# RWKV layers of a five-mixer transformer stack: paired low-rank factors, spread modulation sums, output products split in two

## The chip, the core and the metric

The kernel runs on one NeuronCore of a Trainium2 chip. The metric is the device time of one execution in microseconds (us). TensorE (PE in the profile) multiplies matrices into PSUM, eight banks of 128 partitions by 512 fp32. VectorE (DVE) and ScalarE (ACT) work on tiles of 128 partitions, and both read PSUM. GpSimd (POOL) and SyncE (SP) only issue DMAs here. Each engine works through its own list in order, and semaphores join the lists.

## What is computed

256 tokens of width 1024 go through four layers of feed-forward, mixer, feed-forward, and then through a second block. The mixers are RWKV-7 (layer 0), Mamba-2, windowed attention, and RWKV-7 again (layer 3; called RWKV layer 1 below, `j = 1`). Each of the 12 sublayers is modulated: shift, scale and gate come from `silu(c) @ ada_w`, a product of one row with a 1024 x 3072 matrix per sublayer. The change touches the two RWKV layers:

```python
dx = token_shift(h) - h
xr, xw, xk, xv, xa, xg = [h + dx * mu[j] for j in range(6)]
r = xr @ w_rkv[0];  k = xk @ w_rkv[1];  v = xv @ w_rkv[2]
w = -softplus(-(w0 + tanh(xw @ w1) @ w2)) - 0.5        # w1: 1024x64, w2: 64x1024
decay = exp(-exp(w))
a = sigmoid(a0 + (xa @ a1) @ a2)                       # a1, a2: rank 64
v = v + (v_first - v) * sigmoid(v0 + (xv @ v1) @ v2)   # rank 32, only j = 1
g = sigmoid(xg @ g1) @ g2                              # rank 160
kk = heads(k * k_k);  kk = kk / max(norm(kk), 1e-12)   # 16 heads of 64
k = k * (1 + (a - 1) * k_a)
# per token: state = state*decay + (state @ -kk)(kk*a)^T + v k^T;  y = state @ r
out = ((groupnorm(y) + sum(r*k*r_k) * v) * g) @ w_o
```

## The kernel before, in words

All activations lie transposed, as 8 tiles of 128 channels by 256 tokens. Weights come as 128x128 fp32 blocks, 24 blocks (1.5 MB) to a slot, in the order in which PE uses them, through a ring of three slots that SP fills (`stream_weights`, L397). Modulation weights come on POOL's queue (`ada_stream`, L410): a sublayer takes 16 chunks of 768 KB, there are two buffers, and a chunk is asked for when DVE has summed the one two places before it (`ada_sum`, L421: one 128x1536 multiply-add). RWKV layer 0 has two sublayers' chunks to sum, 32 of them; RWKV layer 1 has none left.

The **product phase** is written by hand on each engine (`rw_products` L931, `rw_act` L1184, `rw_vector` L1317). DVE forms six mixes of `h` and `dx`, 8 tiles each (`mix`, L1332), into two buffers, so mix `i` waits until the products of mix `i-2` are done. PE projects each mix (`project`, L751): 8 products of 128x256 to one output tile, in turn into three PSUM banks, which ACT empties. The order before is k, w1, the sums of squares of the key heads (`key_sums`), a1, the expansions w2 and a2 (`expand`), the spreading of the inverse norms (`spread_norms`), r, v, (v1), g1, (v2), g2. An expansion tile before is one product with 64 rows.

Within r, v and g2 PE also does the first step of a triangular inverse for four units (two chunks of 128 tokens by two halves of the heads): `open_near(u)` makes 128x128 products of the keys, DVE masks and sums them in two rounds (L1380 to L1386), PE replicates each round over the partitions (`spread_near(u, i)`, two 128x512 products), and then DVE runs 15 dependent pairs of small instructions (L1396, L1397). DVE's part is `base(u)`; it ends with the copy at L1398. The phase ends when PE transposes `v` and starts the bonus sums (128x256 products with `head_ones`).

The **chunk phase** goes over b = 0, 1 (chunks of 128 tokens) and hf = 0, 1 (halves of the heads). PE doubles the inverse to 32 and 64 with products of 128x128 (`wk_lx`, `wk_x32`, `wk_y32`, `wk_y64`), and makes the decayed products of r with a (`wk_ra`) and of k with r and kk (`wk_rk`), which DVE masks (L1517, L1520, L1530). Then a chain hands over six times: `wk_res` (PE) to ACT, `wk_sa`, ACT, `wk_across`, DVE (L1541), `wk_sa` again, ACT, and last the output `wk_out`, which for each half of the heads is 8 products k-part times v, 8 products rb times sa, and for b = 1 also 8 of r times state. DVE's L1468 is the first to read the output. `beside(n)` in `rw_vector` places modulation chunks in DVE's list.

Of the kernel before, what the change touches and what calls it, by code (L numbers as in the profile page):

```python
# [21 lines left out]
P = 128  # L22
# [16 lines left out]
RW_SLOTS, MB_SLOTS, SW_SLOTS, B2_SLOTS = 14, 22, 7, 30  # L39
# [39 lines left out]
def weight_slots(v):  # L79
    out = [slots_of([blocks_of(v["ada_w"][0][:, :ADA_COLS])])]  # L80
    for i in range(DEPTH):
        kind, j = i % 3, i // 3
        for s in range(2):
            if s == 1:
                if kind == 0:
                    w_r, w_k, w_v = v["rw_w_rkv"][j]
                    parts = [blocks_of(w_k)]
                    parts += [blocks_of(v[n][j]) for n in ("rw_w1", "rw_a1", "rw_w2", "rw_a2")]
                    parts += [blocks_of(w_r), blocks_of(w_v)]
# [26 lines left out]
    out.append(np.zeros_like(out[0][:-sum(len(o) for o in out) % RING]))  # L116
# [634 lines left out]
def project(k, pe, pr, x, kt, m=P, rows=P, before=None):  # L751

    bank = pr.q % RING
    if pr.q >= RING:
        pe.wait_ge(k.sem["evacuated"], pr.q - RING + 1)
    for t in range(kt):
        if before is not None:
            before(t)
        w = pr.take()
        pr.mm(k.psum[0:m, bank, 0:T], w[0:rows, 0:m], x(t), t == 0, t == kt - 1,  # L760
              k.sem["projected"] if t == kt - 1 else None)
    pr.q += 1

# [88 lines left out]
RW_MIXES = (2, 1, 4, 0, 3, 5)  # L852
# [15 lines left out]
class RwTiles:  # L868


    def __init__(self, k):
# [17 lines left out]
        self.norm = k.rms[0:16, :]  # L889
        self.one_less_ka = k.small[:, 0:8]  # L890
# [40 lines left out]
def rw_products(k, pe, pr, j, n):  # L931
    s, z, tiles = k.sem, RwTiles(k), rw_tiles(j)
    mm, q0 = pr.mm, pr.q
    mixes = iter(range(6))
# [10 lines left out]
    def full(beside=lambda m: None):  # L945
        kw, before = mixed()
        for m in range(KT):
            project(k, pe, pr, before=before if m == 0 else None, **kw)
            beside(m)
        return kw  # L950

    def expand(src, at, rows):
        evacuated(src)
        for m in range(KT):
            project(k, pe, pr, x=lambda t: z.lora[0:rows, at], kt=1, rows=rows)
# [1495 lines left out]
```

## Time and profile before

| | us |
|---|---|
| median of 3 runs | 3614.06 |
| the 3 runs | 3612.92 to 3615.4 |
| the profiled execution | 3613.66 |
| its span, first to last instruction | 3612.0 |
| mean granted TensorE clock, share of full | 0.923 |
| RWKV layer 0, first product of a mix to first product of w_o | 279.29 to 644.89 |
| RWKV layer 1, the same | 2443.84 to 2769.07 |

All times in rows are from the start of the span. The timeline view merges runs of equal instructions: start, duration of the run, engine, line of the kernel, operation, tile written <- tiles read, shapes (rows*columns of the weights, then the moving tile for PE), xcount, and in brackets how long the engine sat idle before and who released it. An fp32 product shows as two MATMUL records, so x16 is eight products.

### The profile page before, as it was taken

How to read it: one execution, taken by the hardware profiler on the slowest of the kernel's cores; microseconds unless marked ns; L12 is line 12 of the kernel's file. 1: busy time of each engine (PE TensorE's matmuls, PEld its weight loads, DVE VectorE, ACT ScalarE, POOL GpSimd, SP SyncE). 2: the span in 40 equal slices, each digit the busy share in tenths (PEclk: the TensorE clock that was granted, in tenths of full speed). 3: DMA queues.
4: the chain of work that ended last, by engine and by line, in shares of the span. 5: the costliest groups of instructions: out<-in, count | busy, mean ns of one | idle time of the engine just before them, and what ended most of it. 6: DMA issues, size and time to landing. Idle time of an engine off the chain costs nothing.

```text
span 3612.0 us, 57308 instructions
## 1 busy us (share of the span) xinstructions
PE 3322.7 (92%) x23680; PEld 3057.3 (85%) x23680; DVE 2050.8 (57%) x2856; ACT 1265.2 (35%) x1895; POOL 93.3 (3%) x180
## 2 busy tenths in 40 slices
PE   7995989999999799999995999999989999997898
PEld 7994768899999777999983899997678998856798
DVE  2656665566656963657655566655752545362444
ACT  2432111334435422435333344344121434331333
POOL 0000000000000000000000000000000000000000
PEclk9997997899999959999995999998897999988999
DMA  7755312465754603766642565752300443421343
GB/s 298 273 200 192 117 69 89 183 240 199 278 218 173 247 1 115 281 233 227 246 164 79 196 240 201 272 191 88 117 1 35 175 179 138 173 110 65 140 179 129
DMA packets 68758, 609.83 MB, mean 169 GB/s; under 512 B 7633, under 2 KB 7665, under 8 KB 30321
## 3 DMA queue, kind: packets, MB, share of 16 engines
q1 hardware_dynamic: 42912, 466.90, 34.5%
q0 software_dynamic: 25344, 138.42, 10.7%
q8 instruction: 126, 2.06, 0.2%
q10 hardware_dynamic: 336, 2.13, 0.1%
q14 instruction: 40, 0.32, 0.0%
HBM read 605.32 MB, written 2.10 MB: 168 GB/s over the span
## 4 chain that ended last, share of the span: by engine, by line
PE 53%; DVE 7%; ACT 2%; issue 1%; DMA 0%; DVEq 0%; ACTq 0%; POOLq 0%
PE psum L272 22%; PE psum L645 21%; PE psum L654 10%; DVE arena L574 1%; DVE rstd L572 1%; ACT arena L516 0%; DVE small L1948 0%; DVE arena L1940 0%; DVE wkv_base L1397 0%; DVE small L1396 0%; ACT up_part L618 0%; DVE arena L1961 0%; DVE h_part L582 0%; DMA ada_in<-in_ada_w 0%; DVE up_part L627 0%
## 5 line engine op out<-in xcount | busy, mean ns | idle before, releaser
L645 PE MATMUL psum<-h_part,up_part 128*128 128x256 f32 x9504 | 1183.0, 285 | 21.2 <-DVE h_part L582 20.4
L645 PEld LDWEIGHTS psum<-h_part,up_part 128*128 128x128 f32 x9504 | 1164.4, 193 | 23.3 <-issue 22.3
L654 PE MATMUL psum<-hidden_part,down_part 128*128 128x256 f32 x4752 | 601.3, 283 | 0.0
L272 PE MATMUL psum<-arena,weights 128*128 128x256 f32 (+3 forms) x2320 | 544.3, 396 | 46.2 <-issue 31.5
L654 PEld LDWEIGHTS psum<-hidden_part,down_part 128*128 128x128 f32 x4752 | 583.9, 192 | 0.0
L272 PEld LDWEIGHTS psum<-arena,weights 128*128 128x128 f32 (+3 forms) x2320 | 443.9, 194 | 149.1 <-issue 58.0
L627 DVE TENSOR_TENSOR up_part<-weights,up_part 128x2048 fp32r<-128x2048 f32 x198 | 453.0, 2288 | 135.4 <-ACT up_part L618 135.4
L618 ACT ACTIVATE up_part<-weights 128x2048 fp32r<-128x2048 f32 x198 | 376.3, 1900 | 42.8 <-DMA weights<-in_weights 41.8
L272 PE MATMUL psum<-arena 128*128 128x128 f32 (+8 forms) x2696 | 361.4, 334 | 27.5 <-DVE arena L1541 7.4
L698 ACT ACTIVATE arena<-psum 128x256 f32<-128x256 f32 x198 | 75.9, 383 | 859.3 <-PE psum L645 859.3
L272 PEld LDWEIGHTS psum<-arena 128*128 128x128 f32 (+3 forms) x2696 | 316.0, 217 | 66.7 <-issue 25.4
L729 DVE TENSOR_TENSOR arena<-arena,psum 128x256 f32<-128x256 f32 x198 | 83.2, 420 | 417.0 <-ACT arena L698 417.0
L272 PE MATMUL psum<-in_part,w_part 128*128 128x256 f32 x2352 | 292.6, 287 | 22.2 <-DVE w_part L793 9.7
L434 DVE SCALAR_TENSOR_TENSOR ada_sum<-ada_in,c_act,ada_sum 128x1536 f32<-128x1536 f32 x154 | 278.5, 1813 | 60.5 <-DMA ada_in<-in_ada_w 56.5
L272 PEld LDWEIGHTS psum<-in_part,w_part 128*128 128x128 f32 x2352 | 289.7, 196 | 25.1 <-issue 23.6
L724 DVE TENSOR_TENSOR down_part<-weights,down_part 128x1024 fp32r<-128x1024 f32 x198 | 241.2, 1218 | 20.6 <-ACT down_part L693 20.6
L272 PE MATMUL psum<-arena,consts 128*128 128x256 f32 (+6 forms) x636 | 195.5, 471 | 38.9 <-DVE small L1398 12.3
L693 ACT ACTIVATE down_part<-weights 128x1024 fp32r<-128x1024 f32 x198 | 206.5, 1043 | 15.1 <-PE psum L654 14.9
L272 PEld LDWEIGHTS psum<-arena,consts 128*128 128x128 f32 (+5 forms) x636 | 119.7, 218 | 96.8 <-issue 23.7
L824 ACT ACTIVATE arena<-psum 128x256 f32<-128x256 f32 (+2 forms) x139 | 54.0, 392 | 351.2 <-PE psum L272 351.2
L793 DVE TENSOR_TENSOR w_part<-weights,w_part 128x1024 fp32r<-128x1024 f32 x98 | 119.1, 1221 | 83.9 <-ACT w_part L787 83.9
L418 POOL DMA_DIRECT2D ada_in<-in_ada_w x174 | 91.9, 528 | 2273.9 <-DVE ada_sum L434 1273.8
(233 smaller groups left out, 1937.0 us busy)
## 6 DMA issues: line engine op xcount, KB each, us to landing
weights<-in_weights SPq DMA_DIRECT2D x294, 1536.0 KB, 6.2
ada_in<-in_ada_w POOLq DMA_DIRECT2D x176, 768.0 KB, 4.7
consts<-in_consts SPq DMA_DIRECT2D x1, 1844.0 KB, 9.3
x<-in_x SPq DMA_DIRECT2D x1, 1024.0 KB, 5.3
v_first<-arena ACTq DMA_DIRECT2D x1, 1024.0 KB, 3.9
arena<-v_first ACTq DMA_DIRECT2D x1, 1024.0 KB, 7.1
out<-x SPq DMA_DIRECT2D x1, 1024.0 KB, 3.9
params<-in_params SPq DMA_DIRECT2D x1, 458.0 KB, 3.3
```

Source lines behind the costliest of these rows:

```text
L272: ins = self.k.nc.tensor.matmul(out, lhsT=w, rhs=x, start=start, stop=stop, is_transpose=turn)
L418: pool.dma_start(k.ada_in[:, b], ada_w[g * 2 + b]).then_inc(k.ada_loaded[b], 16)
L434: ins = k.nc.vector.scalar_tensor_tensor(out, buf, c, out, ALU.mult, ALU.add)
L618: k.nc.scalar.activation(k.up_part[0][:, j % 2], k.weights[:, n % RING, 0:2 * KT * P], ACT.Copy)\
L627: k.nc.vector.tensor_tensor(k.up_part[1][:, j % 2], k.weights[:, n % RING, 0:2 * KT * P], k.up_part[0][:, j % 2].bitcast(FP32), ALU.subtra ...
L645: ins = mm(k.psum[:, j % RING, half * T:(half + 1) * T], lhsT=k.up_part[wp][:, j % 2, b:b + P], rhs=k.h_part[xp][:, t], start=t == 0 and n ...
L654: ins = mm(k.acc[:, d], lhsT=k.down_part[wp][:, j % 2, d * P:(d + 1) * P], rhs=k.hidden_part[xp][:, j % RING], start=start and d % 2 == 0 ...
L693: k.nc.scalar.activation(k.down_part[0][:, j % 2], k.weights[:, (n0 + j) % RING, 2 * KT * P:], copy)\
L698: k.nc.scalar.activation(k.silu[:, j % RING], k.psum[:, j % RING, 0:T], ACT.Silu)\
L724: v.tensor_tensor(k.down_part[1][:, j % 2], k.weights[:, (n0 + j) % RING, 2 * KT * P:], k.down_part[0][:, j % 2].bitcast(FP32), sub).then_ ...
L729: v.tensor_tensor(k.hidden[:, j % RING], k.silu[:, j % RING], k.psum[:, j % RING, T:2 * T], ALU.mult)\
L793: self.k.nc.vector.tensor_tensor(self.k.w_part[1][:, m % RING], self.weights(m)[1], self.k.w_part[0][:, m % RING].bitcast(FP32), ALU.subtr ...
```

## The change

1. `w1` and `a1` become the two column halves of the same 8 blocks, `w2` and `a2` the two row halves of 8 blocks, `v2` rows 32 to 63 of the second row block of `g2`. A RWKV layer takes 13 slots in place of 14. PE starts with `low_ranks` and `decays_and_rates`, which alternate between the halves; then come k, r, v. The two expansion products of an output tile go to two banks, taken as a pair.
2. `spread_norms` makes 8 products with 128 columns in place of 16 with 64, in r after tile 0.
3. The steps of the inverse move: `open_near` and `spread_near` stand at half tiles, unit 1 opens at the end of r, unit 2 in v, unit 3 after v.
4. DVE's modulation chunks of layer 0: before, 16 in one run after the second mix and 16 in the chunk phase. Now 7 between the tiles of k's scaling, 1 after the reciprocal, 3 after `base(0)`, 5 before `base(1)`, and 16 in the chunk phase at other places. In layer 1 `base(3)` goes ahead of the mixing of `v`.
5. Chunk phase: for b = 1 the bank pairs change roles; the k-part times v and the r times state products of the output go between `wk_sa` and `wk_across`, summed in PSUM ahead of rb times sa.

PE's list at the start of RWKV layer 0, before (`arena` holds the mixes, the low-rank results and the keys; `rw_mixed` counts DVE's mix tiles):

```order
L272 MATMUL psum<-arena,weights 128x256 [waits weights_loaded0,rw_mixed]
L272 MATMUL psum<-arena,weights 128x256 [waits rw_mixed] x7
L272 MATMUL psum<-arena,weights 128x256 x16
L272 MATMUL psum<-arena,weights 128x256 [waits weights_loaded1,evacuated]
L272 MATMUL psum<-arena,weights 128x256 x7
```

These are the products of k's first tiles. Now:

```order
L272 MATMUL psum<-arena,weights 64x256 [waits rw_mixed,weights_loaded0]
L272 MATMUL psum<-arena,weights 64x256 [waits rw_mixed] x15
L272 MATMUL psum<-arena,weights 128x256 [waits evacuated] x3
L272 MATMUL psum<-arena,weights 128x256
L272 MATMUL psum<-arena,weights 128x256 [waits evacuated]
L272 MATMUL psum<-arena,weights 128x256
```

The 64 products of k stood first and now stand behind 16 narrow ones and 16 expansions.

DVE's list of layer 0 between the end of `base(0)` (the COPY) and the first step of `base(1)` (the 128x512 TENSOR_TENSOR), before:

```order
L1398 COPY small<-consts 128x1 [waits dve_own]
L1332 SCALAR_TENSOR_TENSOR arena<-arena,params 128x256 [waits projected]
L1332 SCALAR_TENSOR_TENSOR arena<-arena,params 128x256 x7
L1404 SCALAR_TENSOR_TENSOR arena<-arena,params 128x256 [waits evacuated]
L1404 SCALAR_TENSOR_TENSOR arena<-arena,params 128x256 x7
L1407 TENSOR_TENSOR arena<-arena 128x2048 [waits rw_bonus_in]
L1408 TENSOR_TENSOR arena<-arena 128x2048
L1410 COPY small<-consts 128x1 [waits dve_own]
L1380 TENSOR_TENSOR arena<-psum,consts 128x512 [waits wk_near]
```

That is the last mix, the bonus products and two multiplications. Now:

```order
L434 SCALAR_TENSOR_TENSOR ada_sum<-ada_in,c_act,ada_sum 128x1536 [waits ada_summed,ada_loaded0]
L434 SCALAR_TENSOR_TENSOR ada_sum<-ada_in,c_act,ada_sum 128x1536 [waits ada_summed,ada_loaded1]
L434 SCALAR_TENSOR_TENSOR ada_sum<-ada_in,c_act,ada_sum 128x1536 [waits ada_summed,ada_loaded0]
L1378 SCALAR_TENSOR_TENSOR arena<-arena,params 128x256 [waits projected]
...
L1465 COPY small<-consts 128x1 [waits dve_own]
L434 SCALAR_TENSOR_TENSOR ada_sum<-ada_in,c_act,ada_sum 128x1536 [waits ada_summed,ada_loaded1]
L434 SCALAR_TENSOR_TENSOR ada_sum<-ada_in,c_act,ada_sum 128x1536 [waits ada_summed,ada_loaded0]
L434 SCALAR_TENSOR_TENSOR ada_sum<-ada_in,c_act,ada_sum 128x1536 [waits ada_summed,ada_loaded1]
L434 SCALAR_TENSOR_TENSOR ada_sum<-ada_in,c_act,ada_sum 128x1536 [waits ada_summed,ada_loaded0]
L434 SCALAR_TENSOR_TENSOR ada_sum<-ada_in,c_act,ada_sum 128x1536 [waits ada_summed,ada_loaded1]
L1434 TENSOR_TENSOR arena<-psum,consts 128x512 [waits wk_near]
```

Eight chunks now stand between the two. The third place is DVE's list in the chunk phase of layer 0, b = 0, from the mask of `wk_ra` to the read of `wk_across`, before:

```order
L1520 TENSOR_TENSOR arena<-psum,consts 128x1024 [waits wk_ra] x2
L1524 TENSOR_TENSOR arena<-arena,psum 128x1024 [waits wk_y,wk_y64] x2
L1530 TENSOR_TENSOR arena<-psum,consts 128x512 [waits wk_rk]
...
L434 SCALAR_TENSOR_TENSOR ada_sum<-ada_in,c_act,ada_sum 128x1536 [waits ada_summed,ada_loaded0]
L434 SCALAR_TENSOR_TENSOR ada_sum<-ada_in,c_act,ada_sum 128x1536 [waits ada_summed,ada_loaded1]
L1541 TENSOR_TENSOR arena<-arena,psum 64x8x64 [waits wk_res_read,wk_across]
```

Both chunks stand behind all masks. Now:

```order
L431 TENSOR_SCALAR ada_sum<-ada_in,c_act 128x1536 [waits ada_loaded1]
L1572 TENSOR_TENSOR arena<-psum,consts 128x1024 [waits wk_ra]
L434 SCALAR_TENSOR_TENSOR ada_sum<-ada_in,c_act,ada_sum 128x1536 [waits ada_summed,ada_loaded0]
L1572 TENSOR_TENSOR arena<-psum,consts 128x1024 [waits wk_ra]
L434 SCALAR_TENSOR_TENSOR ada_sum<-ada_in,c_act,ada_sum 128x1536 [waits ada_summed,ada_loaded1]
L1577 TENSOR_TENSOR arena<-arena,psum 128x1024 [waits wk_y,wk_y64] x2
...
L434 SCALAR_TENSOR_TENSOR ada_sum<-ada_in,c_act,ada_sum 128x1536 [waits ada_summed,ada_loaded0]
```

Chunks now stand ahead of and between the masks and adds; the last row shown is the one between the two rounds of `wk_rk`. The diff, cut to its core:

```diff
-RW_SLOTS, MB_SLOTS, SW_SLOTS, B2_SLOTS = 14, 22, 7, 30
+RW_SLOTS, MB_SLOTS, SW_SLOTS, B2_SLOTS = 13, 22, 7, 30
-RW_MIXES = (2, 1, 4, 0, 3, 5)
+RW_MIXES = (1, 4, 2, 0, 3, 5)
...
+    def pair():
+        if pr.q >= RING:
+            pe.wait_ge(s["evacuated"], pr.q - RING + 2)
+        banks = pr.q % RING, (pr.q + 1) % RING
+        pr.q += 2
+        return banks
+
+    def low_ranks():
+        banks, w = pair(), pr.take(KT)
+        for t in range(KT):
+            for i in range(2):
+                pe.wait_ge(s["rw_mixed"], 48 * j + KT * i + t + 1)
+                mm(k.psum[z.rows(i), banks[i], 0:T], w[:, t * P + 64 * i:t * P + 64 * i + 64], z.mix[i][:, t],
+                   t == 0, t == KT - 1, s["projected"] if t == KT - 1 else None)
+
+    def decays_and_rates():
         for m in range(KT):
-            project(k, pe, pr, x=lambda t: z.lora[0:rows, at], kt=1, rows=rows)
+            banks, w = pair(), pr.take()
+            for i in range(2):
+                if m == 0:
+                    evacuated(("w1", "a1")[i])
+                mm(k.psum[:, banks[i], 0:T], w[z.rows(i)], z.lora[z.rows(i), 1], True, True, s["projected"])
...
-    def beside_v(m):
-        if m == 2:
+        if (m, half) == (7, 1):
             open_near(1)
-        if m == 4:
+
+    def beside_v(m, half):
+        if (m, half) == (1, 1):
             spread_near(1, 0)
...
         for hf in range(2):
             at("wk_res_read", hf)
             for m in range(8):
-                mm(k.psum[0:64, 4 * hf + 2, m * 64:(m + 1) * 64], z.y[hf][0:64, m, 0:64], z.res[hf][0:64, m],
+                mm(k.psum[0:64, bank(hf, 2), m * 64:(m + 1) * 64], z.y[hf][0:64, m, 0:64], z.res[hf][0:64, m],
                    True, True, s["wk_sa"] if m == 7 else None)
+            for p in range(4):
+                for i in range(2):
+                    part(out(hf, i, p), lhsT=z.kl[hf][:, 4 * i + p, 0], rhs=z.vt[:, b, 4 * hf + p, z.rows(i)],
+                         start=p == 0 and (b == 1 or i == 0), stop=False, skip_group_check=True)
...
     mix(1)
-    if j == 0:
-        for i in range(ADA_STEPS):
-            ada_sum(k, dve, 2, i)
     mix(2)
...
+    for t in range(KT):
+        evacuated("k", t)
+        dve.wait_ge(s["rw_k_factor"], KT * j + t + 1)
+        ins = v.tensor_tensor(z.k[:, t], z.k[:, t], z.k_factor[:, t], mult)
+        if t < KT - 1:
+            beside()
+    ins.then_inc(s["rw_k_scaled"], 1)
+    dve.wait_ge(s["rw_key_sums"], j + 1)
+    v.tensor_scalar(z.norm, k.psum[0:16, 3, 0:T], 1e-24, None, ALU.max).then_inc(s["rw_norm"], 1)
+    mix(4)
+    dve.wait_ge(s["rw_norm_root"], j + 1)
+    v.reciprocal(z.norm, z.norm).then_inc(s["rw_norm"], 1)
+    beside()
```

## Rows read from the trace of the kernel before

**Rows 1.** The page's first line.
```profile
span 3612.0 us, 57308 instructions
```
**Rows 2.** Timeline of PE in the product phase of RWKV layer 0.
```profile
346.18 7.04 PE L272 MATMUL psum<-arena,weights 128*64 128x256 f32 x22 [28.94 <-issue]
...
379.28 1.16 PE L272 MATMUL psum<-arena 64*128 64x128 f32 x16
...
437.14 0.62 PE L272 MATMUL psum<-consts,mod_rows 24*128 24x24 f32 x2 [4.81 <-DVE mod_rows L483]
...
485.09 6.13 PE L272 MATMUL psum<-arena,consts 128*128 128x256 f32 x16 [6.33 <-DVE small L1398]
```
**Rows 3.** Timeline of DVE, modulation chunks of layer 0: first run, second run.
```profile
286.43 1.94 DVE L431 TENSOR_SCALAR ada_sum<-ada_in,c_act 128x1536 f32<-128x1536 f32 x2
...
525.72 3.53 DVE L434 SCALAR_TENSOR_TENSOR ada_sum<-ada_in,c_act,ada_sum 128x1536 f32<-128x1536 f32 x2
...
539.94 1.82 DVE L434 SCALAR_TENSOR_TENSOR ada_sum<-ada_in,c_act,ada_sum 128x1536 f32<-128x1536 f32 x1 [1.33 <-DMA ada_in<-in_ada_w]
```
**Rows 4.** Timelines of layer 0: two narrow PE groups, and ACT emptying expansions.
```profile
313.62 3.63 PE L272 MATMUL psum<-arena,consts 128*16 128x256 f32 x16
...
359.82 3.67 PE L272 MATMUL psum<-rms,consts 16*64 16x256 f32 x32
...
353.46 6.94 ACT L824 ACTIVATE arena<-psum,params 128x256 f32<-128x256 f32 x16
```
**Rows 5.** Stretches: us, busy by engine, then granted PE clock, DMA share, GB/s.
```profile
535.00:545.00 10.00, 6.34 (x60) 6.10 (x60) 6.48 (x7) 0.98 (x2) 1.58 (x3) 0.50 0.56 202
...
2490.00:2500.00 10.00, 10.00 (x34) 6.58 (x34) 7.57 (x12) 6.92 (x16) 0.00 (x0) 0.50 0.00 0
...
2730.00:2740.00 10.00, 10.00 (x98) 9.77 (x98) 1.38 (x2) 2.37 (x4) 0.00 (x0) 0.50 0.01 2
```
**Rows 6.** Timeline of DVE in and after base(0) of layer 0.
```profile
382.27 1.43 DVE L1386 TENSOR_TENSOR arena<-small,consts 128x256 f32<-128x256 f32 x4
...
394.54 0.28 DVE L1396 TENSOR_TENSOR small<-psum,wkv_base 128x120 f32<-128x120 f32 x1 [3.60 <-PE psum L272]
...
402.31 0.15 DVE L1398 COPY small<-consts 128x1 f32<-128x1 f32 x1
402.38 3.25 DVE L1332 SCALAR_TENSOR_TENSOR arena<-arena,params 128x256 f32<-128x256 f32 x8
...
408.83 2.29 DVE L1407 TENSOR_TENSOR arena<-arena 128x2048 f32<-128x2048 f32 x1
```
**Rows 7.** Timeline of PE, three tiles of g2 in layer 0.
```profile
460.90 3.83 PE L272 MATMUL psum<-arena,weights 128*128 128x256 f32 x12 [0.46 <-ACT arena L824]
```
**Rows 8.** Timeline of PE in the product phase of RWKV layer 1.
```profile
2519.34 1.16 PE L272 MATMUL psum<-arena 64*128 64x128 f32 x16
...
2623.97 6.77 PE L272 MATMUL psum<-arena,consts 128*128 128x256 f32 x16 [5.96 <-DVE small L1398]
```
**Rows 9.** Timelines of the chunk phase of layer 1, DVE and PE.
```profile
2660.44 4.86 DVE L1530 TENSOR_TENSOR arena<-psum,consts 128x512 f32<-128x512 f32 x8
...
2761.01 0.69 DVE L1468 TENSOR_REDUCE small<-psum 128x8 f32<-128x512 f32 x1 [8.46 <-PE psum L272]
...
2664.17 21.21 PE L272 MATMUL psum<-arena 128*128 128x64 f32 x288 [1.25 <-DVE arena L1530]
```
**Rows 10.** Timelines of the chunk phase of layer 0, DVE and PE.
```profile
514.04 1.22 DVE L1517 TENSOR_TENSOR arena<-psum,consts 128x1024 f32<-128x1024 f32 x1 [0.56 <-PE psum L272]
...
520.93 4.87 DVE L1530 TENSOR_TENSOR arena<-psum,consts 128x512 f32<-128x512 f32 x8
...
555.32 0.69 DVE L1468 TENSOR_REDUCE small<-psum 128x8 f32<-128x512 f32 x1 [4.05 <-PE psum L272]
...
636.84 0.69 DVE L1468 TENSOR_REDUCE small<-psum 128x8 f32<-128x512 f32 x1 [8.46 <-PE psum L272]
...
538.66 18.60 PE L272 MATMUL psum<-arena 64*64 64x64 f32 x176 [5.41 <-DVE arena L1541]
```

More of the change, by code:

```diff
@@ L745, in ffn_residual_wait, with project @@
     return done
-def project(k, pe, pr, x, kt, m=P, rows=P, before=None):
+def project(k, pe, pr, x, kt, m=P, rows=P, before=None, at=0, beside=lambda half: None):
     bank = pr.q % RING
@@ L966, in spread_norms @@
         for t in range(KT):
-            for i in range(2):
-                mm(k.acc[64 * i:64 * i + 64, t], k.const("ident", 16)[:, 2 * t + i:2 * t + i + 1].to_broadcast([16, 64]),
-                   z.norm, True, True, s["rw_norm_spread"] if t == KT - 1 and i else None)
+            mm(k.acc[:, t], z.norm_rows[:, t * P:(t + 1) * P], z.norm, True, True, s["rw_norm_spread"] if t == KT - 1 else None)
     def near_products(u, bank, signal):
@@ L1169, in rw_products @@
                 for i in range(2):
[L1170 to L1177 removed]
+                    ins = part(out(hf, i, p), lhsT=z.rb[hf][:, 4 * i + p], rhs=z.sa[hf][:, 4 * i + p], start=False,
+                               stop=True, skip_group_check=True)
+            ins.then_inc(s["wk_out"], 1)
     for hf in range(2):
@@ L1237, in rw_act @@
         ev.tile(z.g[:, m], f.Copy)
+        if j:
+            ev.tile(z.v_share[:, m], f.Sigmoid, bias=k.param("rw_v0", m))
     for i in range(4):
@@ L1341, in rw_vector, with beside @@
         mix(0, range(4 * half, 4 * half + 4))
+    units = [(u, i) for u in (2, 3) for i in range(ADA_STEPS)] if j == 0 else []
+    def beside(count=1):
+        for _ in range(count if units else 0):
+            u, i = units.pop(0)
+            ada_sum(k, dve, u, i)
     mix(1)
-    if j == 0:
-        for i in range(ADA_STEPS):
-            ada_sum(k, dve, 2, i)
     mix(2)
-    dve.wait_ge(s["rw_key_sums"], j + 1)
-    v.tensor_scalar(z.norm, k.psum[0:16, 3, 0:T], 1e-24, None, ALU.max).then_inc(s["rw_norm"], 1)
     mix(3)
-    dve.wait_ge(s["rw_norm_root"], j + 1)
-    v.reciprocal(z.norm, z.norm).then_inc(s["rw_norm"], 1)
-    mix(4)
-    evacuated("w2")
+    evacuated("wa2")
     for t in range(KT):
@@ L1400, in rw_vector @@
     base(0)
+    beside(3)
     mix(5)
@@ L1410, in rw_vector @@
     v.tensor_copy(k.small[:, 102:103], k.const("eps")).then_inc(s["rw_keys"], 1)
+    beside(5)
     base(1)
+    base(2)
     if j == 0:
         mod_rows(k, dve, 2)
-    base(2)
-    if j == 0:
-        mod_columns(k, dve, own, 2)
     projected("v1" if j else "v")
@@ L1426, in rw_vector @@
         v.tensor_tensor(z.v, z.v, z.v_first, add).then_inc(s["rw_v_mixed"], 1)
-    base(3)
+    if j == 0:
+        mod_columns(k, dve, own, 2)
     evacuated("v")
@@ L1435, in rw_vector @@
     projected("end")
-    def pair(hf, which):
-        return k.psum[:, 4 * hf + 2 * which:4 * hf + 2 * which + 2, :].rearrange("p i (n c) -> p (i n) c", n=4)
     def each(name, m=8):
         return k.const(name).unsqueeze(1).to_broadcast([P, m, P])
-    chunk = iter(range(ADA_STEPS if j == 0 else 0))
-    def beside(count=1):
-        for _ in range(count):
-            i = next(chunk, None)
-            if i is not None:
-                ada_sum(k, dve, 3, i)
     for b in range(2):
```

256 lines of the change are left out of this document (137 added, 119 removed).

## The prediction, made before the changed kernel ran

> **What bounds the kernel now.** I read the page's first line for the span [rows 1], then the timelines of the two RWKV layers, since everything else keeps its instructions. In a product phase PE sets the end except where it waits for DVE. In layer 0 four such waits matter: 28.94 us before a1's products, because 16 modulation chunks stand in DVE's list ahead of the mix that a1's turn depends on; 4.81 us for the modulation rows; some 3 us at a spread; 6.33 us for the end of `base(3)` [rows 2]. The chunks go at DMA pace: the run begins at 286.43 and takes 59 us for 16 sums of 1.82 us or less [rows 3]. In the chunk phases I compare layer 1, which has no chunks, with layer 0. From the bonus sums to the last `wk_out` layer 1 takes 2761.01 - 2623.97 = 137.0 us [rows 8, 9], layer 0 636.84 - 485.09 = 151.8 us [rows 2, 10]. So 32 chunks cost layer 0 about 29 us in one phase and 14.7 in the other. The question is what they cost at their new places.
>
> **Layer 0, front.** Before, the first near products run at 379.28 [rows 2]. Now: PE can begin `low_ranks` at 279.3, but its second product needs DVE's ninth mix tile, which I put at 283.7 (mix tiles take 3.25/8 = 0.41 us [rows 6]). The 16 products alternate between column halves. That halves run side by side is seen where 16 products into halves take 3.67 us and 8 whole ones 3.63 [rows 4]; bounds are 0.43 us a pair at the high clock and 0.86 at the low one. PE comes from waiting, so I take 0.86: done at 290.7. Tanh, copy and a table load add about 2.2. Then 8 pairs of expansions: ACT needs 6.94/16 = 0.43 us a tile [rows 4], and a pair waits until the tile before last is emptied, so a pair costs 0.43 + 0.05 + (0.43 or 0.86) + 0.1 = 1.0 to 1.44 us; at 1.44 the last is emptied at 304.4, and k's products start at 303.5. They take 27.6 us and 2.5 more for a cold start: 333.6; key sums 3.6.
>
> DVE meanwhile does the cumulative sums (about 10 us) and then the scaling with 7 chunks between. Chunks arrive about 5.3 us after the sum two places earlier, so the loop ends at DMA pace, at 337 to 341; I take 339. From there: 0.5 for the norm, 3.25 for mix 4 [rows 6], 1.73 reciprocal, 3.45 spreading, 24 products of r 10.35: near products at **358.5**, 20.8 us earlier.
>
> **Layer 0, middle.** `base(0)` now takes near 1.2 + first half 3.3 (to the end of the row at 382.27 less 380.4) or the 3.45 of r's tile 4, spread 1.7, half a tile 1.7, spread 1.7, then 7.9 from the first small step to the copy (394.54 to 402.46) [rows 6]: 17.8, so 376.3. Then 3 chunks. A burst with two chunks loaded goes as in the second run: from 525.72 the third sum ends 8.8 us later and the fifth at 541.76, 16.0 us later [rows 3]. So 8.8, then mix 5 3.25, the bonus products 3.25, two multiplications 2.3 each, 11.2 in all [rows 6], then 5 chunks 16.0: `base(1)` starts at 412.3 and its first half is ready at 415.5. PE has done near(1) and two tiles of v by 384.9 and waits for just that: **30.6 us idle**. The wait of 28.94 is not gone but stands at another place. This is the step that I trust most: each length has a row.
>
> From there (S = 415.5): spread, half tile, spread, 20 products, near(2): S + 13.8; `base(2)` ends S + 31.7; v with 24 modulation sums ends S + 34.1; DVE's `ended` and first half of `base(3)` S + 39.6; PE's g1 and transposes S + 43.4; two tiles of g2. A tile of g2 costs 3.83/3 = 1.28 us [rows 7], not 2 x 0.43. Spread(3,0), three tiles, spread(3,1), 8.1 of small steps, modulation columns, transposes: S + 63.9. After the long idle PE runs slow for a while; after a wait of 5.41 us the stretch read 0.50 [rows 5, 10], the lower of the clock's two levels, 1.2 GHz. I add 3. Bonus sums at 482.5, before 485.09 [rows 2]: **-2.6** (range -9 to +3).
>
> Of switching between whole tiles and 32-row halves the Trainium skill ("TensorEngine Tiling (Array Packing)", Key Properties) says that changing the mode drains TensorE. The 1.28 us of rows 7 agrees; without drains 5 tiles would cost 2 us less in each layer.
>
> **Layer 1, product phase.** No chunks. Low ranks bound by DVE's mixes, done at 2451.5; expansions 8.2 to 11.5 (before, with single 64-row products, PE fell to 0.50 in 2490 to 2500 [rows 5]); near products at 2512 to 2518, I take 2515.5, before 2519.34 [rows 8]. `base(0)` 17.8, then 11.2 and 3.3: first spread of unit 1 at 2547.8, while PE is there at 2542: a new wait of about 5.8 us, and 4 us of low clock behind it. Then as above without modulation sums but with v1 (3.6), and with tiles of g2 and v2 in pairs of banks at 1.7 us; `base(3)` ends about 61.2 + 4 later. Only then does DVE mix v, three 128x2048 operations of 2.29 [rows 6], and PE's transposes wait for it. Bonus sums at 2622 to 2626, before 2623.97 [rows 8]: **0** (range -6 to +5). What the shared blocks save (16 expansions to 8 places, 8 products of v2 beside g2's) is lost to the pair rule, the new wait and the later v.
>
> The skill's same page ("PSUM Bottleneck") says that tiling speeds TensorE but not the emptying of PSUM. Rows 4 agree for the expansions: by products alone 8 pairs would be 3.4 us.
>
> **Layer 1, chunk phase.** Does taking a third to two thirds of the output products ahead help? Only if PE waits there. For b = 0 PE's merged row has 288 records in 21.21 us with no idle [rows 9]. By single handovers I find the same: from sa on, ACT and DVE are each done while PE works on the other half of the heads. For b = 1 it is busy 10.00 of 10 at the low clock [rows 5]. The same products in another order end at the same time: **0** (-3 to +1). The swapped banks cost nothing: near(2) no longer waits for the state, but PE is busy until then.
>
> **Layer 0, chunk phase.** Now DVE has one chunk after lx1, two at `wk_ra`, and one between the rounds of `wk_rk`. Before, masks end at 515.26 (lx1) and 525.8 (rk) [rows 10]. Now: 1.0 us chunk, mask, 1.82 chunk, mask at 520.4, chunk 521.5 (its DMA) to 523.3, two adds to 525.7, four rk masks to 528.1, chunk to 529.9, four to 532.3: 6.5 us late. Behind it the chunks between the two across reads are one, not two: before, from the rk masks to the last output 29.5 us (525.8 to 555.32), of which 10.7 are over layer 1's pattern of 18.1 and 0.7 in the start. After: 6.5 + 1 + about 7.5 of low clock, since PE is idle from 526.3 to 531.2 and the wait of 5.41 brought 0.50 before: 15.0, so +4.3 (bounds -3.2 warm, +9.8 all slow). For b = 1: chunks add 7.3 to the end of rk (594.3 to 601.6), and 1.8 of the old delay between the across reads goes: +5.5. Sum **+9.8**.
>
> **Other parts.** Two weight slots fewer: PE waits for no weights in these phases, so 0. Key order, `spread_norms` with 8 products: in the front. The feed-forward layers are unchanged.
>
> **Sum.** -2.6 + 0 + 0 + 9.8 = +7.2 on the profiled 3613.66 (0.4 below the median) gives 3620.9; on the median 3614.06, **3621**.
>
> **Rivals.** *A, the clock holds and DMAs are prompt* (faster): low ranks and expansions at the high clock bring layer 0 -8 and layer 1 -6, the chunk phase 6.5 + 1 - 10.7 + 5.5 = +2.3: 3602. For it: layer 1's b = 0 ran 288 records in 21.21 us, 0.15 us a product, so such products alone do not bring the clock down [rows 9]; against: [rows 5]. *B, the forecast*, with its own range 3612 to 3631. *C, the low clock through* (the other way, slower): from the point at which PE's waits pass about 5 us it stays at 1.2 GHz for the whole handover chain and in g2: layer 0 +2, layer 1 +5, chunk phase +9.8 + 6.5: 3637. *D, the halves do not run side by side* when weights are 128 rows deep: low ranks +6.9 and +3.4, expansions +3.4 to +6.9 in all: 3637 and up; rows 4 speak against it. I make no rival of chunks that are fetched ahead (the 16.0 would be 9.1): there are two buffers, and the third chunk needs a sum to free one.
>
> **How the numbers follow.** A measurement tells about 0.2% (7.2 us) from no change, so the borders are 3606.8 and 3621.3. A 0.20, all faster. B 0.57: 0.32 within, 0.25 slower, since its middle lies at the border. C 0.16 and D 0.07, slower. Together faster 0.20, same 0.32, slower 0.48. The range of 8 in 10 reaches just past the middles of A and C, 3600 to 3639; half of A and half of C and D lie outside.
>
> **What the profile after would show.** A PE wait near 385 to 415 of about 30 us, released by DVE's first step of `base(1)`, in place of the 28.94; in layer 1 the same of 6. Near products of layer 0 at 358. Rk masks of layer 0 ending 6 to 7 us later after `wk_lx`. PE without idle between sa and the output in layer 1, b = 0, and last `wk_out` 137 us after the bonus sums. If the middle wait is under 20 us, or the chunk phase of layer 1 is more than 3 us shorter, my working is wrong.

## The result, and the profile after

The changed kernel takes 3649.97 us (median of 4 runs, 3645.0 to 3653.32); the kernel before took 3613.49 (4 runs, 3611.95 to 3615.4). The ratio is 1.010, 95% interval 1.0082 to 1.0117: slower by some 36 us, where the forecast was 3621 and its range ended at 3639. The profiled execution, the fastest of the four, took 3645.0 us with a span of 3643.3, which is 31.3 over the span of before [rows 1]. By stretch, each from PE's first product of the one step to that of the next:

| stretch | before | after | difference | forecast |
|---|---|---|---|---|
| start to the first mix product of layer 0 | 279.3 | 279.8 | +0.5 | 0 |
| layer 0, to the bonus sums | 205.8 | 216.2 | +10.4 | -2.6 |
| layer 0, bonus sums to `w_o` | 159.8 | 178.7 | +18.9 | +9.8 |
| to the first mix product of layer 1 | 1799.0 | 1794.9 | -4.0 | 0 |
| layer 1, to the bonus sums | 180.1 | 188.0 | +7.9 | 0 |
| layer 1, bonus sums to `w_o` | 145.1 | 143.7 | -1.4 | 0 |
| `w_o` of layer 1 to the end | 842.9 | 841.9 | -1.0 | 0 |

The page of after begins:

```profile
span 3643.3 us, 57258 instructions
```

The timeline of PE in the product phase of layer 0 (columns as ahead of the prediction), which answers to [rows 2]:

```profile
346.48 7.19 PE L272 MATMUL psum<-rms,arena 16*128 16x256 f32 x16 [7.60 <-DVE rms L1421]
353.60 12.54 PE L272 MATMUL psum<-arena,weights 128*128 128x256 f32 x48
366.07 1.16 PE L272 MATMUL psum<-arena 64*128 64x128 f32 x16
384.74 1.16 PE L272 MATMUL psum<-arena 64*128 64x128 f32 x16
...
427.54 3.78 PE L272 MATMUL psum<-arena,consts 128*128 128x512 f32 x4 [34.53 <-DVE arena L1440]
...
496.03 4.33 PE L272 MATMUL psum<-arena,consts 128*128 128x256 f32 x16
```

The 28.94 us wait of before is gone, and one of 34.53 stands behind v's second tile, released by DVE's first step of `base(1)`. What DVE does in that time is in its timeline:

```profile
384.14 3.55 DVE L434 SCALAR_TENSOR_TENSOR ada_sum<-ada_in,c_act,ada_sum 128x1536 f32<-128x1536 f32 x2
396.09 1.82 DVE L434 SCALAR_TENSOR_TENSOR ada_sum<-ada_in,c_act,ada_sum 128x1536 f32<-128x1536 f32 x1 [8.40 <-DMA ada_in<-in_ada_w]
397.83 3.25 DVE L1378 SCALAR_TENSOR_TENSOR arena<-arena,params 128x256 f32<-128x256 f32 x8
...
408.88 3.55 DVE L434 SCALAR_TENSOR_TENSOR ada_sum<-ada_in,c_act,ada_sum 128x1536 f32<-128x1536 f32 x2
415.79 1.82 DVE L434 SCALAR_TENSOR_TENSOR ada_sum<-ada_in,c_act,ada_sum 128x1536 f32<-128x1536 f32 x1 [3.36 <-DMA ada_in<-in_ada_w]
```

These are eight chunks on a path on which PE waits: 13.7 us for three of them and 15.4 for five.

In the chunk phase of layer 0, b = 0, the timelines of DVE and PE around the masks of `wk_rk`, to be held against [rows 10]:

```profile
530.48 1.82 DVE L434 SCALAR_TENSOR_TENSOR ada_sum<-ada_in,c_act,ada_sum 128x1536 f32<-128x1536 f32 x1 [1.16 <-DMA ada_in<-in_ada_w]
532.21 2.35 DVE L1577 TENSOR_TENSOR arena<-arena,psum 128x1024 f32<-128x1024 f32 x2
534.47 2.48 DVE L1583 TENSOR_TENSOR arena<-psum,consts 128x512 f32<-128x512 f32 x4
536.87 1.81 DVE L434 SCALAR_TENSOR_TENSOR ada_sum<-ada_in,c_act,ada_sum 128x1536 f32<-128x1536 f32 x1
538.59 2.48 DVE L1583 TENSOR_TENSOR arena<-psum,consts 128x512 f32<-128x512 f32 x4
```

```profile
533.48 2.87 PE L272 MATMUL psum<-arena 64*128 64x256 f32 x16 [2.66 <-DVE arena L1577]
539.93 8.99 PE L272 MATMUL psum<-arena 128*128 128x64 f32 x48 [3.58 <-DVE arena L1583]
548.85 3.67 PE L1187 MATMUL psum<-arena 128*128 128x64 f32 x16
```

The last line is the value part, now ahead of `wk_across`. The stretches give the granted clock (columns as in [rows 5]):

```profile
534.00:541.00 7.00, 3.42 (x19) 2.19 (x16) 7.00 (x11) 0.00 (x0) 0.53 (x1) 0.57 0.41 130
541.00:577.00 36.00, 35.69 (x259) 34.32 (x260) 12.20 (x26) 4.84 (x9) 1.58 (x3) 0.50 0.25 85
```

PE is busy 35.69 of 36.00 us at 0.50 of full clock. In layer 1, b = 0, where no chunk stands, products of the same kinds run at 1.00:

```profile
2694.94:2716.00 21.06, 21.06 (x278) 20.38 (x280) 8.53 (x26) 5.04 (x10) 0.00 (x0) 1.00 0.01 2
```

### The profile page after: what moved, and what is told of

The parts are those of the page before. It is cut to its first block, busy times and chain, and to the rows that moved or that the text cites. A ratio compares the mean times of both kernels' runs of the same rounds, so it can differ in the third digit from the quotient of the medians.

```text
span 3643.3 us, 57258 instructions
## 1 busy us (share of the span) xinstructions
PE 3323.1 (91%) x23648; PEld 3056.1 (84%) x23648; DVE 2053.4 (56%) x2870; ACT 1266.4 (35%) x1897; POOL 93.4 (3%) x180
## 4 chain that ended last, share of the span: by engine, by line
PE 53%; DVE 6%; ACT 2%; issue 1%; DMA 0%; DVEq 0%; ACTq 0%; POOLq 0%
PE psum L272 21%; PE psum L645 21%; PE psum L654 10%; DVE arena L574 1%; DVE rstd L572 1%; ACT arena L516 0%; DVE small L2001 0%; DVE arena L1993 0%; PE psum L1187 0%; PE psum L1214 0%; ACT up_part L618 0%; DVE arena L2014 0%; DVE h_part L582 0%; DVE arena L1378 0%; DMA ada_in<-in_ada_w 0%
## 5 line engine op out<-in xcount | busy, mean ns | idle before, releaser
L272 PE MATMUL psum<-arena,weights 128*128 128x256 f32 (+2 forms) x2320 | 530.4, 400 | 34.1 <-DVE arena L1378 17.2
L272 PEld LDWEIGHTS psum<-arena,weights 128*128 128x128 f32 (+2 forms) x2320 | 429.5, 195 | 138.6 <-issue 36.8
L272 PE MATMUL psum<-arena 128*128 128x128 f32 (+8 forms) x2376 | 315.4, 334 | 29.7 <-DVE arena L1583 9.6
L272 PEld LDWEIGHTS psum<-arena 128*128 128x128 f32 (+3 forms) x2376 | 270.3, 214 | 67.4 <-issue 23.4
L827 ACT ACTIVATE arena<-psum 128x256 f32<-128x256 f32 (+3 forms) x136 | 53.2, 393 | 424.3 <-PE psum L272 424.3
```

Source lines behind the costliest of these rows:

```text
L272: ins = self.k.nc.tensor.matmul(out, lhsT=w, rhs=x, start=start, stop=stop, is_transpose=turn)
```

## The experiments

There are two theories on the whole of the difference. **P**: the places of the 32 chunks in DVE's list cost most of it. **S** or **V**: the new structure does (halves and shared blocks, the later mixing of `v`; in the chunk phase the value part summed early and the swapped banks). Each kernel's marks come from PE's timeline of its profiled execution: "L0 near" and "L0 bonus" are the starts of layer 0's first near products and of its bonus sums in us from the start of the span, the next three columns are durations.

| kernel | span | L0 near | L0 bonus | L0 bonus to `w_o` | L1 first to bonus | L1 bonus to `w_o` | median (range) of its runs |
|---|---|---|---|---|---|---|---|
| before | 3612.0 | 379.3 | 485.1 | 159.8 | 180.1 | 145.1 | 3613.5 (3612.0 to 3615.4) |
| after | 3643.3 | 366.1 | 496.0 | 178.7 | 188.0 | 143.7 | 3650.0 (3645.0 to 3653.3) |
| n_before | 3560.6 | 348.2 | 454.1 | 145.0 | 177.9 | 145.0 | 3570.9 (3555.9 to 3584.5) |
| n_after | 3580.9 | 357.2 | 458.3 | 145.8 | 188.0 | 146.2 | 3579.6 (3577.8 to 3592.4) |
| place | 3626.1 | 365.5 | 496.0 | 159.2 | 188.0 | 143.7 | 3627.8 (3624.1 to 3631.5) |
| late | 3644.8 | 367.8 | 497.9 | 174.3 | 188.0 | 144.3 | 3643.3 (3640.4 to 3646.5) |
| late_place | 3629.9 | 366.6 | 496.7 | 161.8 | 188.0 | 144.3 | 3630.5 (3624.9 to 3633.1) |
| inbase | 3623.1 | 366.6 | 477.2 | 176.5 | 187.9 | 143.7 | 3628.8 (3624.8 to 3634.3) |
| mixpair | 3640.2 | 363.6 | 493.8 | 178.1 | 186.2 | 143.7 | 3645.0 (3641.9 to 3646.6) |
| b_place | 3641.2 | 381.2 | 487.0 | 173.7 | 179.9 | 159.3 | 3642.9 (3637.8 to 3652.2) |
| best1 | 3597.4 | 363.7 | 467.0 | 159.2 | 179.8 | 143.9 | 3592.5 (3588.6 to 3599.1) |
| b_best | 3599.8 | 356.1 | 459.0 | 164.8 | 174.5 | 159.1 | 3598.1 (3581.3 to 3601.4) |
| best2 | 3592.8 | 353.8 | 457.0 | 156.8 | 177.1 | 160.9 | 3594.5 (3581.2 to 3596.4) |
| before_2 | 3605.7 | 380.0 | 485.8 | 164.2 | 171.3 | 145.0 | (one run) 3607.4 |

The kernel before ran again beside each later group of kernels, with medians of 3618.2, 3614.3, 3625.3 and 3611.6 and single runs from 3604 to 3653. That spread is wider than what most single edits are worth, so the edits are judged by the marks, and the reason of the spread has a part of its own below. The marks scatter too: in two executions of the same kernel (`before`, `before_2`) layer 0's chunk phase differs by 4.4 us and layer 1's product phase by 8.8.

**The chunks taken out of both kernels.**

```diff
-    if unit >= NORMS:
+    if unit >= NORMS or unit in (2, 3):
         return
```

Units above 3 move down by two in the stream and in the waits. Both kernels leave out the modulation of two sublayers.

> The changed kernel with the 32 modulation chunks of RWKV layer 0 left out: neither fetched nor summed, so the modulation of two sublayers is wrong and the time is that of the rest. Theory P (the chunks' places are the main cause): layer 0 then looks like layer 1; the 34.53 us wait falls to about 6, the chunk phase from the bonus sums to the first product of w_o falls from 178.7 to about 144, and the front ends at ACT's and PE's pace; span about 3575. Rival S (the new structure is the cause: column halves, shared banks, the later mixing of v, the early value sums): the span stays 25 us or more above that of the same removal in the kernel before.

> The kernel before with the same 32 chunks left out (same part of the computation missing). Theory P: the 28.94 us wait goes and the chunk phase falls from 159.8 to about 145: span about 3568, so the two kernels without chunks differ by 5 to 13 us, which is what layer 1 shows (+6.5) once more or less. Rival S: they differ by 25 us or more.

From layer 0's first product to its `w_o` `n_before` and `n_after` take some 320 and 325 us, 5 apart; with chunks they are 29.3 apart (10.4 + 18.9). So the chunks' places cost some 24 of layer 0's 29, as P has it. The middle wait of PE in `n_after` is 6.14 us, as in layer 1 of after:

```profile
390.32 3.78 PE L272 MATMUL psum<-arena,consts 128*128 128x512 f32 x4 [6.14 <-DVE arena L1442]
```

S is not nothing, though. Layer 1 of `n_after` is 11.3 us longer than that of `n_before` (188.0 + 146.2 against 177.9 + 145.0), and the spans are 20.3 apart, more than the 5 to 13 expected, while the medians are 8.7 apart; two of the four runs of `n_before` (3579.5 and 3584.5) lie 17 us or more above the other two. The structure costs 5 in layer 0 and 6.5 to 11 in layer 1; of the rest of the 20.3, 4 lie outside the two layers, where no instruction differs.

**The chunk phase: places against early sums.** `place` puts the chunks back, `late` sums the value part at the end, `late_place` does both, and `b_place` gives the kernel before the new places alone.

```diff
-        beside()            # behind both first masks
+            beside()        # behind each
...
-            beside()        # behind each mask of wk_ra; one more behind the second wk_lx
...
-            beside()        # behind each round of wk_rk
+        beside(2)           # behind both rounds
...
-            beside()        # behind each across read
+            beside(2)
```

> The changed kernel with DVE's 16 chunks of the chunk phase put back where they stood before (one after each first mask, two behind all rk masks, two after each across read); the product phase and PE's order stay as changed. Theory P: from the bonus sums to the first product of w_o 178.7 falls to 160 to 163, the PE wait of 2.66 ahead of the last rk products is gone; span 3625 to 3628. Rival V (the value part summed early and the swapped banks are the cause in this phase, because PE stays at the lower clock): less than 4 us gained, 3640 to 3645.

> The changed kernel with the value part of the outputs (and r times state) summed at the end of the chain as before; the chunks stay at their new places. Theory P: within 3 us of the changed kernel (3640 to 3648), since PE has the same products and is busy or is waiting for masks that are late. Rival V: layer 0's phase falls by 9 or more, span 3635 or less.

> The kernel before with one part of the change alone: DVE's 16 chunks of the chunk phase at the places of the changed kernel. Theory P: from the bonus sums to the first product of w_o of layer 0 159.8 rises to 170 to 178, span 3622 to 3630. Rival V (these places cost only together with the value part summed early): less than 4 us.

> The changed kernel with both parts of its chunk phase undone: chunks at the old places and the value part of the outputs summed at the end of the chain. Against the run with the old places alone it shows what the early sums are worth where DVE's masks are on time. Theory E0 (PE is busy or slow there anyway, the order of the same products is worth nothing): bonus sums to first product of w_o 158 to 162 in place of 159.2. Rival E1 (the early sums fill the waits for the across reads, 3.16 and 2.04 us): 163 to 166, and layer 1 unchanged at 144.

The phase falls from 178.7 to 159.2 with the old places and rises from 159.8 to 173.7 when the kernel before gets the new ones: P, in both directions. The span of `b_place`, 3641.2, still missed the 3622 to 3630 expected, because layer 1's chunk phase took 159.3 us in it where it took 145.1 (below).

The worth of the early sums is less clear. `late` ends at 174.3, 4.4 us less than after; its span is 1.5 above that of after, its median 6.7 below. At the old places `late_place` takes 161.8 against 159.2, in the range of E0 (158 to 162) and not in that of E1. PE's timeline of `late_place` and then of `place` around the wait for the across reads shows the mechanism that E1 named:

```profile
548.55 23.64 PE L272 MATMUL psum<-arena 64*64 64x64 f32 x176 [5.75 <-DVE arena L1589]
```

```profile
543.38 3.07 PE L272 MATMUL psum<-arena 64*64 64x64 f32 x48
549.61 3.92 PE L272 MATMUL psum<-arena 64*64 64x64 f32 x48 [3.16 <-DVE arena L1592]
```

The sums fill 2.6 us of a wait of 5.75. That the net 2.6 is the same 2.6 is not shown. In b = 0, from the first product of `wk_rk` to the end of the output, `place` takes 32.4 us and `late_place` 38.0, but the two executions of the kernel before, which sum late, take 32.6 and 37.4, and in b = 1 `place` loses 2.8 us again. Over the whole phase the three executions with early sums at the old places (`place`, `best1`, `best2`) take 156.8 to 159.2 and the four with late sums (`before`, `before_2`, `late_place`, `b_best`) 159.8 to 164.8. So the early sums probably bring something where DVE's masks are on time; how much is open. In layer 1 the two kernels are 0.6 us apart.

**The middle of the product phase.** `inbase` puts the eight chunks where DVE waits inside `base`:

```diff
             if i:
+                beside((2, 2, 1, 0)[u])
                 dve.wait_ge(s["wk_spread"], 2 * UNITS * j + 2 * u + 1)
...
         own.of(v.tensor_copy(x, k.const("same_row").unsqueeze(1).to_broadcast([P, 8, 16])))
+        beside((1, 1, 1, 0)[u])
...
     base(0)
-    beside(3)
...
-    beside(5)
     base(1)
```

> The changed kernel with the eight chunks between base(0) and base(1) put inside base(0), base(1) and base(2), where DVE waits for PE to spread a round (three, three and two chunks); nothing else moved. Theory P: PE's wait ahead of the first spread of unit 1 falls from 34.53 us to 5 to 9, as in RWKV layer 1 (6.14), bonus sums of layer 0 at 466 to 472 in place of 496.03, span 3614 to 3620. Rival M (the chunks then wait for their DMA inside base and lengthen it by as much): bonus sums after 480, span 3627 or more.

PE's wait falls from 34.53 to 5.88, and the bonus sums come 18.9 us earlier, at 477.2, between the ranges of P (466 to 472) and M (after 480); the span, 3623.1, lies between theirs too. PE's timeline:

```profile
405.57 3.65 PE L272 MATMUL psum<-arena,consts 128*128 128x512 f32 x4 [5.88 <-DVE arena L1441]
```

The timeline of DVE shows the price:

```profile
372.65 3.55 DVE L434 SCALAR_TENSOR_TENSOR ada_sum<-ada_in,c_act,ada_sum 128x1536 f32<-128x1536 f32 x2
376.11 1.42 DVE L1441 TENSOR_TENSOR arena<-small,consts 128x256 f32<-128x256 f32 x4
381.72 1.82 DVE L434 SCALAR_TENSOR_TENSOR ada_sum<-ada_in,c_act,ada_sum 128x1536 f32<-128x1536 f32 x1 [4.05 <-issue]
```

With half tiles DVE waited only 0.58 and 2.01 us inside `base(0)` of the changed kernel, less than the 5.4 of three sums, and the third chunk, which POOL asked for at 375.12, comes 6.6 us later. `base(0)` takes 23.5 us in place of 16.9, `base(1)` 21.5 in place of 19.1, `base(2)` 18.0 in place of 16.8. M was half right: the chunks lengthen base, but by 10 us in all, where ahead of `base(1)` they took 29.

**The front.** `mixpair` makes the first two mixes in turn:

```diff
-        mix(0, range(4 * half, 4 * half + 4))
+        for t in range(4 * half, 4 * half + 4):
+            mix(0, (t,))
+            mix(1, (t,))
```

> The changed kernel with DVE making the first two mixes tile by tile in turn, so that PE's alternating low-rank products do not wait for the ninth of 16 mix tiles. Theory L (the late second product costs the front of both layers): low ranks of layer 1 done 3 to 4 us earlier and its bonus sums too; layer 0 gains 0 to 3, since its k loop ends at DMA pace; span 3636 to 3641. Rival C (the front is bound by the granted clock and by ACT): less than 1 us in either layer, span 3642 to 3645.

Counted from the layer's first product, the low ranks are done 2.7 us sooner in layer 0 and 1.8 in layer 1. The near products gain the same, 2.8 and 1.9, and so do layer 1's bonus sums, 1.9 (expected 3 to 4). So L is right in kind and too large: the late second product costs layer 1 some 2 us of its 7.9. The span is 3.1 shorter, the end of the expected range that lies nearest to no gain.

**Towards a faster kernel.** `best1` joins `place`, `inbase` and `mixpair`, lets `base(1)`, the last mix and `base(2)` follow `base(0)` directly, and spreads the norms a tile later. `best2` also moves the front chunks. `b_best` leaves the kernel before as it is but for the product-phase chunks (and `mod_sums`, which needs them):

```diff
-        for i in range(ADA_STEPS):
-            ada_sum(k, dve, 2, i)
+    early_sums(8)           # behind mix(1); 2 more behind mix(4), 3 in base(0), 3 in base(1)
```

> The changed kernel with what the runs so far point to: the chunk-phase chunks at the places of before, the eight middle ones inside base as in the run above, base(1) and base(2) directly behind base(0) with the last mix between, the first two mixes in turn, spread_norms one tile of r later. Theory P: bonus sums of layer 0 at 455 to 463, of layer 1 12 to 15 us earlier than in the changed kernel relative to its first product, chunk phase 159, span 3582 to 3595, faster than both kernels. Rival D (DVE becomes the bound, since bonus products and two multiplications now stand ahead of base(3)): bonus sums of layer 0 at 470 or later, span 3600 to 3612.

> The kernel before with nothing but its product-phase chunks moved in DVE's list: 8 behind the second mix in place of 16, 2 behind mix 4, 3 inside each of base(0) and base(1), where DVE waits for a spread; mod_sums and the turn of the modulation rows stand later in v. Theory P (where the chunks stand is worth more than all the rest of the change): the wait of 28.94 falls to 0 to 5, near products of layer 0 at 350 to 356, bonus sums at 458 to 466, span 3583 to 3593, level with the best version built on the changed kernel. Rival S (the shared blocks and the half-tile places bring something by themselves): 3600 or more.

> The best version so far with its front chunks moved: 3 behind the fourth mix, where DVE waited 8.5 us for ACT, 3 in the k loop in place of 7, 2 behind the reciprocal. Theory Q (the k loop ended at DMA pace, with waits of 4.1, 1.2, 4.9 and 4.6 us in it): the loop ends with the products of k, near products of layer 0 at 357 to 360 in place of 363.65, and the span falls by 3 to 6. Rival R (the two chunks behind the reciprocal take what the loop gives): within 2 us.

`best1` takes 3592.54 us, 0.992 of before (0.989 to 0.996): bonus sums of layer 0 at 467.0 (P had 455 to 463), layer 1's 8.2 us earlier (12 to 15 expected); the span, 3597.4, is 2 over the expected range. `best2` takes 3594.51 (0.991, 0.988 to 0.994) and `b_best` 3598.06 (0.992, 0.989 to 0.995). The lowest runs of the two are 3581.2 and 3581.3. The span of `b_best`, 3599.8, missed P's range (3583 to 3593) and is just under S's 3600, but 14 us of it are layer 1's chunk phase again (159.1 against 145.0), and its bonus sums at 459.0 are in P's range. So nothing here shows that the shared blocks, halves and early sums bring anything that the kernel before does not get from moving its chunks alone. In `best2` the k loop no longer holds PE: near products at 353.8 against 363.7, more than the 4 to 7 that Q had; the span falls by 4.6 only, because layer 1's chunk phase took 17.1 us more in this execution (below).

> The kernel before, unchanged, profiled once more, to see where its runs differ by up to 30 us. Theory K: one of the stretches of 128x64 and 64x64 products runs at the lower clock where it ran at the higher one in the first profile, with the same instructions and no wait more; each such stretch is worth 10 to 15 us. Rival: a longer wait for a DMA.

K is right on the mechanism: the waits of PE and DVE on DMAs are the same in kind, and 69.8 us in `before_2` against 71.5 in `before`. Its layer 1 reaches the bonus sums 8.8 us sooner, because products that ran at 0.50 now run near 1.00. The expansions of w2 and a2 in PE's timeline of `before` and then of `before_2`:

```profile
2485.89 10.60 PE L272 MATMUL psum<-arena,weights 64*128 64x256 f32 x26 [0.76 <-ACT arena L824]
```

```profile
2491.28 5.90 PE L272 MATMUL psum<-arena,weights 64*128 64x256 f32 x26 [0.77 <-ACT arena L824]
```

This is not a stretch of the kind that K named, and is worth 6.6 us up to the near products. One of that kind went the other way: the 176 records of 64x64 products that took 18.60 us in `before` [rows 10] take 23.40 in `before_2` (its timeline), and layer 0's chunk phase is 4.4 us longer (164.2 against 159.8).

```profile
539.23 23.40 PE L272 MATMUL psum<-arena 64*64 64x64 f32 x176 [5.36 <-DVE arena L1541]
```

Phases without any change of code therefore move by 4 to 9 us in both directions.

## Why the prediction was wrong, step by step

- **Direction.** Slower was the likelier sign and the likelier mechanism: a wait that only changes its place [rows 2]. The forecast had the wait at 30.6 us and the rest nearly even. The time is outside the range: the span grew by 31.3 us, not by 7.2. Of the 24.1 between them the front of layer 0 makes 7.6, its middle 4.4, the chain behind it 1.5, its chunk phase 9.1, layer 1's product phase 7.9, and the rest, where next to nothing was forecast, takes 6.4 off.
- **Front of layer 0, near products at 358.5; measured 366.1.** Low ranks (done at 290.4 against 290.7), key sums (335.2 against 337.2) and the end of the k loop (340.9 against 339) were right. Then PE waited 7.60 us for the reciprocal, and I gave the spreading after it 3.45 us and the 24 products 10.35: they took 7.19, at a granted clock of 0.50, and 12.54. The step that failed is that I charged a cold start to the middle and none to this wait. That is 5.9 of the 7.6 us by which the near products were late; nearly all the rest is the k loop (1.9).
- **Middle of layer 0.** The step "I trust most" held in kind. The wait is 34.53, not 30.6: three chunks took 13.7, not 8.8, because the third waited 8.40 us for its DMA, and five took 15.4, not 16.0. I had taken one burst [rows 3] as the pattern. The trace of after gives, for the ten chunks of 340 to 430:

```profile
DMA to landing us min/median/max: 4.3/4.5/9.6
```

  One late landing is 5 us on this path. Behind it the chain took 68.5 us against the 67 forecast. In all the bonus sums are 13.5 us later than forecast: 7.6 from the front, 4.4 here, 1.5 in the chain.
- **Chunk phase of layer 0, +9.8; measured +18.9.** The late masks were sized well: from the end of the masks of the second `wk_lx` to that of `wk_rk` 6.1 us more (6.5 forecast), and for b = 1, from the last output of b = 0 to the end of the `wk_rk` masks, 7.6 more (7.3). The term for the clock failed: from the `wk_rk` masks of b = 0 to the last output it took 35.3 us against the 29.5 of before, where my terms come to 27.3 (29.5 - 10.7 + 1 + 7.5), with PE slow for part of it. It stayed at 0.50 for all 36 us. Even my bound "all slow" was too low: it puts 13.0 us in place of the 7.5, and with it the stretch comes to 32.8. The bonus sums at the start of the phase took 1.8 us less, which I had not forecast, and b = 1 lost 1.1 us behind its masks where I had taken 1.8 off. The 35.3 is no accident of one execution, since `mixpair` and `inbase`, with the same chunk phase, measure 35.3 as well; but the kernel before measures 32.8 in `before_2`, so part of the 5.8 us over it is its own scatter.
- **Layer 1, 0; measured +7.9.** The new wait was right, 6.14 us against 5.8. What failed is the front. The second low-rank product waited 3.80 us for the ninth mix tile, so that the low ranks were done 9.6 us after the first product, not 7.7; k's products, partly at the lower clock, took 30.5 us where I had reckoned 27.6 at the higher; and near products came at +77.9, not +71.7. From there to the bonus sums it took 110.1 against 108.5, of which 9.26 are a wait for the mixing of `v` by DVE. PE's timeline of after for the two waits:

```profile
2474.07 6.36 PE L272 MATMUL psum<-arena,weights 128*64 128x256 f32 x34 [3.80 <-DVE arena L1378]
...
2654.23 3.64 PE L272 MATMUL psum<-consts,arena 128*128 128x128 f32 x16 [9.26 <-DVE arena L1481]
```

  `mixpair` shows that the first is worth some 2 us. No run moves the mixing of `v` alone, so what the second costs is open.
- **Chunk phase of layer 1, 0; measured -1.4**, though the bonus sums, at a higher clock, took 2.9 less (3.83 us in place of 6.77). The total is inside the -3 to +1; the rest alone is 1.5 longer, just outside. In b = 0 PE had no idle between sa and the output. This step and its reason hold.
- **Rivals.** C (the low clock through, 3637) was the right mechanism in layer 0's chunk phase, but I left the DMA wait and the front out of it. Its "+5 in layer 1" came from somewhere else. A reason that I gave for rival A does not hold: one stretch of 288 records at the full clock does not show that such products alone leave the clock up. The same 288 ran at 0.54 in `b_place` (below). D is refuted. The timeline and the stretch of the low ranks of layer 0:

```profile
284.25 7.28 PE L272 MATMUL psum<-arena,weights 128*64 128x256 f32 x34 [3.33 <-DVE arena L1378]
```

```profile
284.25:291.50 7.25, 7.20 (x34) 3.90 (x34) 4.22 (x11) 1.46 (x3) 0.00 (x0) 0.66 0.00 0
```

  The 34 records are the last 30 of the low ranks and the first 4 of the expansions: 0.214 us a record at 0.66 of the clock, where the 128x16 products of [rows 4] take 0.227 at 1.00 (3.63 for 16). At one clock the difference is plain: from 284.30 to 289.00 there are 23 records of halves in 4.70 us at 0.50, and in layer 1, from 2492.90 to 2497.20, 12 records of k's whole products in 4.30 us, also at 0.50. The Trainium skill ("TensorEngine Tiling (Array Packing)", Key Properties) says that tiles operate independently and in parallel; the trace agrees, with these numbers.
- **The drain at a change of mode.** No run isolates it. In the trace of [rows 7] 0.31 to 0.32 us pass from one record to the next between the two records of one product too, where nothing changes, so the 1.28 us a tile do not show a drain.
- **Other parts, 0; measured +0.5, -4.0 and -1.0** where no instruction changed. A single profiled execution does not settle such differences.

## What to carry to other kernels

Work that fills an engine's idle time is free only where that engine waits anyway: write down for each place who is queued behind it, and sum the whole burst at the DMA's worst landing in the trace, not at its typical one. When a wait disappears, ask which path takes its place before asking how much is gained; here eight 1.8 us sums moved from one critical path to another. And put the lower clock as a bound on every phase of small products, whether a new wait of PE stands ahead of it or not: here one phase took 8.0 us more than forecast by it, and another 15 us with no new wait at all.

## What the runs showed of the hardware

The granted clock can fall while PE is busy. In layer 1, b = 0, the kernel before has 288 records in 21.21 us [rows 9]. `b_place` has the same instructions in that layer; its timeline, and the stretch:

```profile
2677.33 36.12 PE L272 MATMUL psum<-arena 128*128 128x64 f32 x288 [1.25 <-DVE arena L1532]
```

```profile
2677.00:2713.00 36.00, 35.67 (x286) 34.97 (x288) 9.96 (x28) 6.04 (x11) 0.00 (x0) 0.54 0.00 1
```

PE is busy 35.67 of 36.00 us as the profile counts it, hardly a DMA runs (0.00 share), the wait ahead is 1.25 us in both kernels, and the clock is 0.54 here and 1.00 there. That is 15 us that nothing in this layer's code explains. `b_best` shows it too (its timeline):

```profile
2635.63 36.01 PE L272 MATMUL psum<-arena 128*128 128x64 f32 x288 [1.25 <-DVE arena L1539]
```

and so does `best2`, whose layer 1 takes 160.9 us from bonus sums to `w_o` where `best1` takes 143.9. The Trainium skill ("TensorE: Matmul & The Clock Gate", Part 1) ties the lower clock to idle time and says that activity releases it. These stretches of 128x64 and 64x64 fp32 products do not agree: activity of 35.67 in 36.00 us did not release it.

The clock also explains the spread of the runs in part. The runs of `b_best` fall into two groups, 3581 to 3586 and 3598 to 3601, those of `best2` into 3581 to 3582 and 3594 to 3596, some 17 and 14 us apart, and one such stretch is worth 15; both profiled executions, which have it slow, belong to the upper group. That the lower groups have it fast was not seen, since no run of theirs was profiled. What decides which clock a stretch gets was not settled: in layer 1 the code, the wait ahead and the DMA share are the same. An edit of this size must be judged by several runs or by marks inside a trace, and a difference of under 15 us between two single runs of such a kernel says little.
